# Who subtracts the low half of the weights: VectorE for both halves of a unit, GpSimd for none

## What is computed

```python
def encoder_layer(x, ...):
    h = x @ w_in                                  # (tokens, 1024) @ (1024, 2912)
    (a_q, a_k, a_v, a_g, b_cq, b_ckv, b_kr, b_g, c_q, c_k, c_v, c_g) = jnp.split(h, split_at, axis=-1)
    oa = window_attn(a_q, a_k, a_v, sink, t5_table) * jax.nn.silu(a_g)
    ob = mla(b_cq, b_ckv, b_kr, w_uq, ...) * jax.nn.silu(b_g)
    oc = neighborhood_attn(c_q, c_k, c_v, rpb) * jax.nn.silu(c_g)
    o = jnp.concatenate([oa, ob, oc], axis=-1) @ w_out      # (tokens, 1024) @ (1024, 1024)
    return layer_norm(DEEPNORM_ALPHA * x + o, ln_g, ln_b)

def trunk(x, ...):
    x = layer_norm(x, ln_in_g, ln_in_b)
    for l in range(DEPTH):                        # 2
        x = encoder_layer(x, ...)
    return x
```

## Time and profile before

| what | value |
|---|---|
| median of 3 runs | 1842.55 us (1841.69 to 1842.91) |
| the profiled execution, its own time | 1846.45 us |
| its span, first to last instruction | 1844.7 us |
| TensorE busy | 1798.5 us (97%) |
| VectorE busy | 945.6 us (51%) |
| ScalarE busy | 772.2 us (42%) |
| GpSimd busy | 431.5 us (23%) |
| mean granted TensorE clock | 0.997 of full |

### The profile page before, as it was taken

The page is one execution under the profiler, slowest core; times in us unless marked ns, Lnnn a source line. Parts: engine busy times, 40 slices in busy tenths (PEclk is TensorE's granted clock), DMA queues, the critical chain, the costliest instruction groups (busy, mean ns, idle before and its releaser), DMA issues.

```text
span 1844.7 us, 32212 instructions
## 1 busy us (share of the span) xinstructions
PE 1798.5 (97%) x12530; PEld 1467.1 (80%) x12530; DVE 945.6 (51%) x2060; ACT 772.2 (42%) x1666; POOL 431.5 (23%) x668
## 2 busy tenths in 40 slices
PE   4999999999999999999999999999999999999997
PEld 4887689889987666889989866988898766578897
DVE  6365765211425776555463476550133277565638
ACT  2345754211125666553233366441212366755510
POOL 0353402311111273001162223140111224600010
PEclk9999999999999999999999999999999999999999
DMA  6676332211124122004145552521212061200022
GB/s 232 174 248 173 107 126 92 92 46 47 47 69 124 27 65 80 1 1 149 35 155 160 155 139 70 183 92 37 67 47 69 23 149 40 95 12 2 24 81 92
DMA packets 148308, 167.16 MB, mean 91 GB/s; under 512 B 18320, under 2 KB 134416, under 8 KB 147648
## 3 DMA queue, kind: packets, MB, share of 16 engines
q1 hardware_dynamic: 145792, 157.64, 28.6%
q0 software_dynamic: 1152, 4.19, 0.6%
q10 hardware_dynamic: 1216, 3.28, 0.5%
HBM read 143.00 MB, written 32.65 MB: 95 GB/s over the span
## 4 chain that ended last, share of the span: by engine, by line
PE 91%; DVE 6%; ACT 1%; issue 1%; DMA 1%; POOL 0%; SPq 0%; DVEq 0%
PE psum L633 66%; PE psum L758 8%; PE psum L728 8%; PE psum L710 6%; DVE nmax L1147 2%; PE psum L769 1%; DVE pt_sb L1178 1%; PE psum L643 1%; DMA w_stage<-w_in 1%; PE psum L615 0%; POOL gT L1405 0%; DVE w_lo L517 0%; PE psum L596 0%; ACT w_stage L898 0%; DVE x_lo L1138 0%
## 5 line engine op out<-in xcount | busy, mean ns | idle before, releaser
L633 PE MATMUL psum<-w_hi,x_hi 128*128 128x256 f32 (+1 forms) x1344 | 380.9, 283 | 3.3 <-DVE x_lo L1138 3.3
L633 PE MATMUL psum<-w_hi,x_lo 128*128 128x256 f32 (+1 forms) x1344 | 379.2, 282 | 0.0
L633 PE MATMUL psum<-w_lo,x_hi 128*128 128x256 f32 (+1 forms) x1344 | 376.8, 280 | 0.0
L633 PE MATMUL psum<-x_hi,w_hi 128*128 128x512 f32 x816 | 325.5, 399 | 0.5 <-POOL w_lo L517 0.5
L633 PE MATMUL psum<-x_lo,w_hi 128*128 128x512 f32 x816 | 324.4, 398 | 0.0
L633 PE MATMUL psum<-x_hi,w_lo 128*128 128x512 f32 x816 | 324.4, 398 | 0.0
L517 POOL TENSOR_TENSOR w_lo<-w_stage,w_hi 128x1024 fp32r<-128x1024 f32 (+1 forms) x79 | 159.2, 2023 | 685.9 <-ACT w_hi L929 685.8
L517 DVE TENSOR_TENSOR w_lo<-w_stage,w_hi 128x1024 fp32r<-128x1024 f32 (+1 forms) x81 | 139.1, 1734 | 298.9 <-ACT w_hi L929 298.9
L633 PEld LDWEIGHTS psum<-w_hi,x_hi 128*128 128x128 f32 x1344 | 254.3, 189 | 3.9 <-DVE x_lo L1138 3.7
L633 PEld LDWEIGHTS psum<-w_lo,x_hi 128*128 128x128 f32 x1344 | 256.4, 191 | 0.2
L633 PEld LDWEIGHTS psum<-w_hi,x_lo 128*128 128x128 f32 x1344 | 253.5, 189 | 0.0
(11 more groups left out here) (148 smaller groups left out, 2602.2 us busy)
## 6 DMA issues: line engine op xcount, KB each, us to landing
w_stage<-w_in SPq DMA_DIRECT2D x48, 512.0 KB, 4.4
w_stage<-w_in SPq DMA_DIRECT2D x88, 256.0 KB, 3.4
toep<-rpb_tile SPq DMA_DIRECT2D x12, 1152.0 KB, 15.5
rpb_tile<-rpb_col SPq DMA_DIRECT2D x48, 192.0 KB
hT<-y SPq DMA_DIRECT2D x18, 512.0 KB, 5.5
y<-hT SPq DMA_DIRECT2D x18, 512.0 KB, 2.7
w_stage<-w_out SPq DMA_DIRECT2D x32, 256.0 KB, 4.1
w_stage<-w_out SPq DMA_DIRECT2D x16, 512.0 KB, 5.3
```

Of the source, the lines that this page charges most:

```text
L633: last = nc.tensor.matmul(out, w, x, start=(n == 0 and part != 1), stop=(n == len(pairs) - 1 and part != 0))
```

## The change

VectorE does both halves of every unit and GpSimd none. Where VectorE subtracted half 1, it now subtracts half 0 and half 1, one behind the other, at the same place of its order. GpSimd's subtractions are taken out of its order, and two pieces of its bias rows, which stood before and behind a subtraction, become one.

```diff
                 else:
                     norm_coef((ln_stat, ln_sqrt, ln_coef), ln_no[s - 1, NTILES[s - 1] - 1] - 1)
                     tail_gain(s - 1, 2)
-                    split_low(dve, s, 1, 1)
+                    for hf in range(2):
+                        split_low(dve, s, 1, hf)
                     tail_gain(s - 1, 1)
                     tail_gain(s - 1, 0)
                 for i, u in enumerate(in_units(s)):
                     if i:
-                        split_low(dve, s, i + 1, 1)
+                        for hf in range(2):
+                            split_low(dve, s, i + 1, hf)
...
                     if s == 0 and i == 0:
-                        split_low(dve, s, 1, 1)
+                        for hf in range(2):
+                            split_low(dve, s, 1, hf)
...
                     if t == 0 and n in (1, 2):
-                        split_low(dve, s, NI + n + 1, 1)
+                        for hf in range(2):
+                            split_low(dve, s, NI + n + 1, hf)
                     if (n, t) == (0, 0):
-                        split_low(dve, s, NU - 3, 1)
+                        for hf in range(2):
+                            split_low(dve, s, NU - 3, hf)
...
                     if (n, t) == (3, NT - 3) and s + 1 < RUNS:
-                        split_low(dve, s + 1, 0, 1)
+                        for hf in range(2):
+                            split_low(dve, s + 1, 0, hf)
...
                 for i in range(NI):
-                    if i > 1 or (s == 0 and i == 1):
-                        split_low(pool, s, i, 0)
                     if s and i == 1:
-                        split_low(pool, s, i, 0)
                         bias_rows(s - 1, range(NTILES[s - 1] - 3, NTILES[s - 1]))
...
-                split_low(pool, s, NI, 0)
                 U = units_of("AC", s)
...
-                for i in range(NI + 1, NU):
-                    split_low(pool, s, i, 0)
                 if s + 1 < RUNS:
                     pool.wait_ge(lnp_loaded, 32 * (s + 1))
-                    bias_rows(s, range(max(NT - 5, 0)))
-                    split_low(pool, s + 1, 0, 0)
-                    bias_rows(s, range(max(NT - 5, 0), NT - 3))
+                    bias_rows(s, range(NT - 3))
```

## The result

The changed kernel takes 1846.37 us (median of 16 executions, 1845.37 to 1848.29), the kernel before 1842.53 us (median of 16, 1841.69 to 1846.1). The ratio is 1.0016, with a 95% interval of 1.0009 to 1.0023: 3.0 us slower, between 1.7 and 4.2. The interval excludes a ratio of 1, but the difference is still under the 0.2% that the forecast took as what a measurement of this kernel can tell. The medians themselves lie 3.8 us apart. The forecast was 1.9 us slower, 1844.4 us, with a range up to 1847.0.

What follows compares the result with a forecast made beforehand. TensorE, busy 97% of the span, was taken to bound the kernel. Terms 1.13 + 1.2 - 0.47 = +1.86 us on the median 1842.55 gave 1844.4 us, range 1841.9 to 1847.0.

Steps and rivals of the forecast that it cites:

- The price of a subtraction: VectorE's weight subtractions: 88 of 1024 and 72 of 512 elements would cost about 154 us instead of 139.1.
- The alone price: VectorE subtracting without GpSimd beside it: 1.18 us per 1024 elements and 0.70 us per 512.
- The start: First pass, pause before L809: both `ck` halves now stand behind the last `tc` copy, so TensorE resumes 1.13 us later.
- the rival of the third pass: Start of third pass: bias rows get in between, `aq0` 1.1 us late, `aq1` still late; 1846.0 us, chance 0.11.
- the clock stays low longer: After the longer pause before L809, the 6.8 us half-speed stretch lasts twice as long, costing 3.4 us; 1847.8 us, chance 0.10.
- The banks: Output projection, second and fourth pass: tile 0's addition waits behind two subtractions, making tile 4 of `o0` 0.6 us late each.
- The third pass: Start of third pass: `aq1` no longer waits for GpSimd's half behind two bias rows, a gain of 0.47 us.
- the nearest row: GpSimd's 4.63 us subtraction, waiting through VectorE's back-to-back instructions, was taken as the model for `aq0`, giving -0.47 us.
- The rest at nothing: GpSimd's other work and VectorE's subtractions at the ends of the first and third pass were priced at no cost.
- A real gain: Rival: under 1838.9 us, needing TensorE to wait 3.7 us for GpSimd's subtractions, where it waits 0.5; chance 0.02.
- nothing is lost: Rival: 0.57 us of the start's loss returns through the clock and output projection additions are on time; 1842.5 us, chance 0.20.

Runs made afterwards that it cites:

- mends three places: Changed kernel with `ck` subtractions before the `tc` copies, `o0` tile 0 added before `o1` subtractions, `aq0` pieces before the gain multiplication: 1840.91 us, again 1840.69 us.
- the kernel before once more: The kernel before, run again with a profile and no edit: 1842.63 us, ratio 0.9995.

## Why the prediction was right, and where it fell short

**The price of a subtraction was right.** The alone price, 1.18 and 0.70 us, gave 154 us; it came to 159.4, by means of 1.23 and 0.82 us, far from the means of before. Of the 88, 86 took 1.21 to 1.23 us, and of the 72, 67 took 0.68 to 0.69; four of the others took 2.9 us each, all beside a bias row of GpSimd, as at `aq0`. What did not follow is VectorE's busy time, forecast 15 us up and measured 4.9 us down, because the rest of its work got shorter (last section).

**The start was right in its length and lacked its second half.** Forecast +1.13, measured +1.14 us. The failed step is the one that came next to it: the forecast took the half-clock stretch of the profile as a part of the kernel before, that would be there after the change too, and so priced the clock at nothing. The experiments show that most executions of before have no such stretch and that the longer pause brings one: +1.52 us in the profile, most of the gap between the forecast 1.9 us and the 3.8 us between the medians. That the time fell into the range all the same is in part luck: its upper edge, 1847.0 us, was set by the rival of the third pass and 1 us for another place, not by the clock. The rival "the clock stays low longer" looked at the right place with the wrong condition: it asked for a stretch longer than 6.8 us, while a stretch of 3.4 us where there had been none was enough. There was a sign: the profiled execution took 3.9 us more than the median, and the forecast only subtracted that difference instead of asking where it was in the trace. Half of 6.8 us is 3.4 of it.

**The banks were right.** Forecast 2 x 0.6 us, measured 0.63 and 0.64, and 1.1 us came back when the addition went first.

**The third pass was half right.** The forecast was -0.47 us, its rival +1.1 with `aq1` late as before. Both mechanisms showed: the wait at `aq1` went (-0.58 us) and the bias row came in between at `aq0` (+0.41 us). The failed step is the choice of the nearest row: GpSimd was shut out through a row of VectorE's instructions at 849 us, and here it got its turn at once. The sum is -0.17 us.

**The rest at nothing** held: no further wait of TensorE in the changed kernel names a subtraction. Two small terms were not foreseen: +0.25 us in the dense attention of the fourth pass, where the waits for VectorE's copy (L1178) are 6.5 us in sum instead of 6.1, in the changed kernel and most made from it, but 6.9 and 6.4 us also in the two made from the kernel before with one and two subtractions moved; and 0.2 us around the span, which is 1.75 to 1.84 us in all profiles of kernels where GpSimd keeps 77 subtractions or more, and 1.95 to 2.05 us where it has none or one. Neither was traced to a cause.

**"A real gain" and "nothing is lost"** did not come. Of the second, the idea that a part of the loss comes back through the clock was the wrong way round.

## What to carry to other kernels

Where the profiled execution's own time lies well above the median, find in its trace what the others don't have before taking its rows as the kernel; here it was a half-clock stretch, and about one execution in four took that long. A pause of TensorE is to be priced with what it does to the clock behind it, 1.1 us more of a pause cost 2.7 us here between two profiles, and two subtractions put ahead of four copies took the pause and the half clock away. And before work is moved from one engine to another everywhere, ask at which places an engine waits for it: here it was two of 79, and the kernel that moves only those two, one of them put earlier, was as fast as the one that moves all 79 and mends three places (1841.0 and 1840.7 us).

## What the hardware showed that was not expected

VectorE did 79 more subtractions and was busy 4.9 us less. Its subtractions took 20 us more, so all else took 25 us less. The groups by shape of two lines that the change doesn't touch, in the kernel before once more and in the changed one:

```profile
L1289 DVE CUSTOM_DVE_ANT_0 rope_k<-hT 128x192 f32<-128x192 f32 x24 | 13.0, 540 | 1.2
L1307 DVE TENSOR_SCALAR hT<-hT,rms 128x192 f32<-128x192 f32 x24 | 12.5, 522 | 0.1
```

```profile
L1292 DVE CUSTOM_DVE_ANT_0 rope_k<-hT 128x192 f32<-128x192 f32 x24 | 8.6, 358 | 1.2
L1310 DVE TENSOR_SCALAR hT<-hT,rms 128x192 f32<-128x192 f32 x24 | 7.6, 318 | 0.1
```

540 became 358 ns and 522 became 318 ns: a few of these small instructions had been waiting behind GpSimd's long subtractions, as VectorE's own subtractions had. The longest of them, in the kernel before once more, with the subtraction of GpSimd beside it:

```profile
131.20 2.40 POOL L517 TENSOR_TENSOR w_lo<-w_stage,w_hi 128x1024 fp32r<-128x1024 f32 x1 [3.38 <-ACT w_hi L929]
131.25 2.47 DVE L1307 TENSOR_SCALAR hT<-hT,rms 128x192 f32<-128x192 f32 x1
```

It starts 0.05 us behind GpSimd's and ends 0.12 us after it, and took 2.47 us, where its group takes 0.32 on average in the changed kernel. The Trainium skill ("SBUF — State Buffer", in its list of port rules) says that the two engines exclude each other for a whole instruction, the later one fully blocked, where VectorE's is in a two-port mode or has two SBUF inputs while GpSimd's reads SBUF. The 2.47 us agree with the blocking; in which mode L1307 ran, no run here shows. The forecast used that rule for the subtractions alone and forgot VectorE's other work. The waits cost no time that is seen here: no wait of TensorE names these lines.

The first products of an execution change their pace in the same way: in the profile of before they follow every 0.21 us until 26.0 us and every 0.12 us from 26.24 on, and in that of the changed kernel the step comes at 23.8 us. That it is the clock is not shown, since the view's granted clock reads 1.00 on both sides of the step. Between the two profiles of before this stretch makes about 1 us.
